# Joined key weights, wider complex products and an earlier token and modulation load in a one-core diffusion trunk

## The reference, cut to what matters

```python
def even_mixer(u_ctx, u_lat, w_in, w_out, ...):
    z = u @ w_in                                  # 27 tiles of 128 columns
    hyena: v, x1, x2 = conv3(z[:1536])            # two long convolutions by DFT:
        y = x1 * irfft(rfft(v) * rfft(filter_0))
        y = x2 * irfft(rfft(y) * rfft(filter_1))
    rwkv, 8 heads of 64, forward and backward over the tokens:
        S = S * w_t + (S @ -kk_t) outer (kk_t * a_t) + v_t outer k_t
        out_t = S @ r_t
    return concat(hyena, readout(rwkv)) @ w_out
```

## Time and profile before

| | |
|---|---|
| executions timed, median | 2153.88 us |
| the profiled execution | 2149.79 us, span 2148.0 us |
| mean granted TensorE clock | 0.973 |
| busy: TensorE, weight load, VectorE, ScalarE, GpSimd | 94%, 76%, 37%, 35%, 43% |
| first chunk products to first SwiGLU product | 34.6 to 72.5 us |
| even mixer's recurrence with its preparation | 684 to 867 us |

### The profile page before, as it was taken

How to read it: one execution, slowest core, us unless ns; L and a number is a source line. 1 busy time by engine, 2 the same in 40 slices (tenths; PEclk the granted TensorE clock), 3 DMA queues, 4 the chain that set the end, 5 groups by cost and what they waited for, 6 DMA issues and landing times.

```text
span 2148.0 us, 32168 instructions
## 1 busy us (share of the span) xinstructions
PE 2023.6 (94%) x13777; PEld 1621.7 (76%) x13777; DVE 799.1 (37%) x1158; ACT 752.2 (35%) x1060; POOL 919.4 (43%) x423
## 2 busy tenths in 40 slices
PE   5999999989999688889999998999999989989997
PEld 2677877768864577667788776777888869979996
DVE  3332032262237654363212224522133346546113
ACT  1512222254344332562222124522122275545343
POOL 0443443435413320443344444444444454448884
PEclk9999999999999799899999999999999999999998
DMA  9564336323320334326533543463232232225551
GB/s 323 181 210 153 119 106 223 121 79 137 108 49 12 73 71 104 132 94 206 195 108 108 196 157 108 133 223 124 79 118 78 69 124 79 80 79 157 196 182 55
DMA packets 232190, 276.53 MB, mean 129 GB/s; under 512 B 46725, under 2 KB 201491, under 8 KB 231732
## 3 DMA queue, kind: packets, MB, share of 16 engines
q1 hardware_dynamic: 228730, 268.65, 38.4%
q10 hardware_dynamic: 3322, 5.86, 0.8%
HBM read 265.05 MB, written 9.44 MB: 128 GB/s over the span
## 4 chain that ended last, share of the span: by engine, by line
PE 82%; DVE 6%; ACT 4%; issue 3%; DMA 2%; SPq 2%; POOL 1%; ACTq 0%; POOLq 0%; DVEq 0%
PE psum L1247 82%; DMA arena<-in_ada_w 1%; DMA arena<-in_x 1%; DVE rs L2087 1%; ACT arena L883 1%; SPq L672 0%; ACTq L795 0%; DVE h L2066 0%; ACT w_hi L854 0%; ACT L945 0%; DMA arena<-v_kept 0%; DVE arena L2175 0%; SPq L658 0%; ACT arena L1195 0%; DVE h L2134 0%
## 5 line engine op out<-in xcount | busy, mean ns | idle before, releaser
L2565 POOL TENSOR_TENSOR w_lo<-arena,w_hi 128x1024 fp32r<-128x1024 f32 x332 | 815.1, 2461 | 1011.5 <-ACT w_hi L854 1009.3
L1247 PE MATMUL psum<-u_hi,w_hi 128*128 128x512 f32 (+1 forms) x1888 | 699.3, 370 | 38.5 <-ACT u_hi L883 15.2
L1247 PE MATMUL psum<-u_hi,w_lo 128*128 128x512 f32 (+1 forms) x1888 | 689.5, 365 | 0.0
L1247 PE MATMUL psum<-u_lo,w_hi 128*128 128x512 f32 (+1 forms) x1888 | 675.2, 363 | 0.0
L854 ACT ACTIVATE w_hi<-arena 128x1024 fp32r<-128x1024 f32 x332 | 349.1, 1058 | 728.1 <-PE psum L1247 717.6
L1247 PEld LDWEIGHTS psum<-u_hi,w_hi 128*128 128x128 f32 x1888 | 363.1, 192 | 130.9 <-issue 28.6
L1247 PEld LDWEIGHTS psum<-u_hi,w_lo 128*128 128x128 f32 x1888 | 363.4, 192 | 54.7
L1247 PEld LDWEIGHTS psum<-u_lo,w_hi 128*128 128x128 f32 x1888 | 359.3, 191 | 53.4 <-issue 0.5
L2036 DVE TENSOR_TENSOR tmp<-psum,tmp 128x512 f32<-128x512 f32 (+1 forms) x88 | 55.0, 625 | 585.0 <-ACT tmp L908 585.0
L1247 PE MATMUL psum<-hid_hi,w_hi 128*128 128x512 f32 (+1 forms) x704 | 257.4, 366 | 1.7 <-POOL w_lo L2565 1.2
L1247 PE MATMUL psum<-hid_hi,w_lo 128*128 128x512 f32 (+1 forms) x704 | 255.3, 363 | 0.0
(11 more groups left out here) (259 smaller groups left out, 1478.8 us busy)
## 6 DMA issues: line engine op xcount, KB each, us to landing
arena<-in_ada_w SPq DMA_DIRECT2D x48, 1536.0 KB, 6.9
arena<-in_ffn_wg SPq DMA_DIRECT2D x44, 1024.0 KB, 5.5
arena<-in_ffn_wu SPq DMA_DIRECT2D x44, 1024.0 KB, 8.0
arena<-in_ffn_wd SPq DMA_DIRECT2D x20, 2048.0 KB, 8.8
arena<-in_ev_w_in SPq DMA_DIRECT2D x6, 2048.0 KB, 7.8
arena<-in_od_w_in SPq DMA_DIRECT2D x6, 2048.0 KB, 8.6
arena<-in_ffn_wd SPq DMA_DIRECT2D x4, 1024.0 KB, 5.0
arena<-inverse_kept SPq DMA_DIRECT2D x32, 128.0 KB, 3.0
```

Of the source, the lines that this page charges most:

```text
L1247: return pe.matmul(dst, w, x, start=first_, stop=last, skip_group_check=True)
L2565: pool.tensor_tensor(piece_shape(split_lo(pc), src), src, piece_shape(split_hi(pc).bitcast(F32), src), ALU.subtract).then_inc(S("lo_done"), 1)
```

## The change

It has five parts.

1. Loads: the token blocks are issued by SP, two at its very head and two behind the filter network's inputs; all eight modulation chunks are issued ahead of the first up weights. ScalarE issues the constants after its first sine, copies five token tiles, does the second sine, three more tiles and then the Silu of `c`; `ada_out(0)` goes ahead of `first_pieces`. TensorE makes `taps_of(1)` after two chunks in place of three.
2. Complex products: six operations of 128x1024 in place of twelve of 128x512.
3. Keys: both kinds lie side by side (`key_pairs`, two buffers each), so that one weight load has 128 columns. `both_kinds` has 8 matmuls in place of 16, `turn_keys` 16 in place of 32. The writers work on 64 partitions each (`key_slot`, `halves_of`): four operations for what two did. The values get a third buffer.
4. Decays are split in "keys" and "read" parts, those of pair 1 have homes of their own; the copy of the first rates goes (`rates` writes to `aa` itself).
5. Order: `strict(1)` comes ahead of `both_kinds(0, 0)`, which waits for it; `strict(2)` in step 0 and `strict(3)` at the end of step 2, in place of steps 1 and 3. `lanes(1)` is split over the doublings and step 0. The rates of pair 1 come before `lanes(0)`. SP's list of moves follows.

```diff
@@ the start: SP, ScalarE, TensorE
+            load_tokens(0)
+            load_tokens(1)
             load_filter("ld_mlp", zT, K["k_zT"])
...
             load_filter("ld_mlp", fw2, A["hy_f_w2"][0])
-            load_ada(0, 0)
+            load_tokens(2)
+            load_tokens(3)
...
-            for c in range(1, 6):
+            for c in range(AN):
                 load_ada(0, c)
             sp.wait_ge(S("ada_used"), 3)
             load_up("up_a", 0, 0, 0)
-            load_ada(0, 6)
-            load_ada(0, 7)
...
+            for k in range(KT):
+                if k == TOK_RING:
+                    act.wait_ge(S("sin_arg"), 2)
+                    act.activation(h2, pre, ACT.Sin).then_inc(S("sin_done"), 1)
+                act.wait_ge(S("tok_turned"), k + 1)
+                act.activation(hv[:, k], bank[1 + k % TOK_RING], ACT.Copy).then_inc(S("h_ready"), 1)
...
+            ada_out(0)
             first_pieces(0, 0, PIECES)
-            ada_out(0)
...
             ada(0, 1)
+            taps_of(1)
             ada(0, 2)
-            taps_of(1)
@@ VectorE, multiplied
+                    re, im = psum[:, 4 * s:4 * s + 2, :], psum[:, 4 * s + 2:4 * s + 4, :]
...
+                    ve.tensor_tensor(out_re, re, kre, ALU.mult).then_inc(S("ve_steps"), v.step())
+                    ve.tensor_tensor(ft, im, kim, ALU.mult).then_inc(S("ve_steps"), v.step())
+                    ve.tensor_tensor(out_im, re, kim, ALU.mult).then_inc(S("ve_steps"), v.step())
+                    ve.tensor_tensor(im, im, kre2, ALU.mult).then_inc(S("ve_steps"), v.step())
+                    ve.wait_ge(S("ve_steps"), v.n)
+                    ve.tensor_tensor(out_re, out_re, ft, ALU.subtract).then_inc(S("ve_steps"), v.step())
+                    ve.tensor_tensor(out_im, out_im, im, ALU.add).then_inc(S("ve_steps"), v.step())
@@ keys
-        bk0 = [by_tile(at) for at in (h[:, 0:1024], h[:, 1024:2048])]
-        bk1 = by_tile(h[:, 2048:3072])
+        key_pairs = [at.rearrange("p d c (i k t) -> p d c i k t", i=2, k=2)
+                     for at in (h[:, 0:2048].rearrange("p (d c x) -> p d c x", d=2, c=CT),
+                                big[:, 0:4096].rearrange("p (d c x) -> p d c x", d=2, c=CT)[:, :, :, 0:256])]
...
+        def key_slot(j, d, kind, e):
+
+            return key_pairs[j % 2][rows_of[e], d][:, :, :, kind ^ e]
...
                     for c in range(CT):
-                        for kind, key in enumerate((bk0[j % 2], bk1)):
-                            for e, rows in enumerate(rows_of):
-                                ins = mm(bank[factor_bank(n, d, e)][rows_of[e ^ kind], c * P:(c + 1) * P], key[rows, d, c, t],
-                                         two_kinds(rows, ar0[j % 3][:, d, c, t], ar1[j % 2][:, d, c, t]), True, True)
+                        for e, rows in enumerate(rows_of):
+                            ins = mm(bank[factor_bank(n, d, e)][:, c * P:(c + 1) * P], both_keys(d, c, n, rows),
+                                     two_kinds(rows, ar0[j % 3][:, d, c, t], ar1[j % 2][:, d, c, t]), True, True)
@@ both_kinds, waits of d == 0
-                        pe.wait_ge(S("a_done"), min(STEPS, n + 2 + n % 2) if n else 2)
-                        pe.wait_ge(S("slots_1"), 2 + 4 * j)
+                        pe.wait_ge(S("a_done"), 4 if n < 2 else 6 if n < 5 else 8)
+                        pe.wait_ge(S("slots_1"), 6 + 6 * j)
@@ GpSimd
+                pool.wait_ge(S("h_moves"), 144)
+                pool.wait_ge(S("bonus_k"), 4)
+                second_keys(0)
                 reads(0)
-                pool.wait_ge(S("h_moves"), 144)
                 pool.wait_ge(S("first_slots"), 7)
                 receives(1)
-                pool.wait_ge(S("rates"), 1)
-                pool.wait_ge(S("slots_0"), 4)
+                second_keys(1)
+                reads(1)
+                pool.wait_ge(S("first_slots"), 9)
+                pool.wait_ge(S("slots_0"), 6)
+                pool.wait_ge(S("zeroed"), 7)
                 pool.memset(arena[:, 2048:4096], 0.0).then_inc(S("zeroed"), 1)
@@ TensorE, VectorE: order of the steps
-                strict(1)
                 both_kinds(1, 0)
...
                     if ahead:
                         turn_keys(n + 2)
+                    if n == 0:
+                        strict(2)
...
-                lanes(0)
                 rates(0, 1, 2)
                 rates(1, 0, 1)
                 ve.wait_ge(S("ve_steps"), v.n)
                 ve.sem_inc(S("first_slots"), 1)
+                lanes(0)
@@ SP, values
-                if n >= 2:
-                    sp.wait_ge(S("o_mm"), n - 1)
+                if n >= 3:
+                    sp.wait_ge(S("o_mm"), n - 2)
+                elif n == 2:
+                    sp.wait_ge(S("slots_0"), 6)
```

More of the change, by code:

```diff
@@ L1037, in even_mixer @@
                 act.activation(chunk_decay, big[:, 0:4096].rearrange("p (x t) -> p x t", t=C)[:, :, C - 1], ACT.Exp, scale=-DECAY).then_inc(S("exped"), 1)
-                decays_of(0, 0)
-                decays_of(0, 1)
+                for part in ("keys", "read"):
+                    for d in range(2):
+                        decays_of(0, d, part)
+                for d in range(2):
+                    decays_of(1, d, "keys")
                 v_out(0)
@@ L1089, in even_mixer @@
                 keys_out(1)
-                act.wait_ge(S("zeroed"), 6)
+                act.wait_ge(S("zeroed"), 7)
                 z_out(0, 4)
+                for d in range(2):
+                    decays_of(2, d, "read")
                 z_out(0, 5)
                 act.wait_ge(S("hy_done"), 4)
-                act.wait_ge(S("first_slots"), 9)
-                act.activation(aa[0], a_first, ACT.Copy).then_inc(S("rates"), 1)
                 for n in range(STEPS):
@@ L1103, in even_mixer @@
                         z_out(n + 1, 4)
-                        if n in (0, 2):
-                            decays_of(n // 2 + 2, 0)
+                        if n in (1, 2):
+                            for d in range(2):
+                                decays_of(3, d, "keys" if n == 1 else "read")
                         z_out(n + 1, 5)
@@ L1575, in bonus_sum @@
                     mm(bank[SPARE[i]], blk[:, :], bonus[:, i * NT:(i + 1) * NT], True, True).then_inc(S("bonus_sum"), 1)
+                bonus_sum(0)
+                bonus_sum(1)
+                pe.wait_ge(S("hy_mul"), 4)
+                back_turned(1)
                 v_turn(2)
                 v_turn(3)
-                for i in range(4):
-                    bonus_sum(i)
+                bonus_sum(2)
+                bonus_sum(3)
+                strict(1)
                 def both_kinds(n, d):
@@ L2241, in even_mixer @@
                     ve.tensor_tensor(ar0[0][:, d], chunk(kk, ch), recv, ALU.mult).then_inc(S("first_slots"), 1)
-                    ve.tensor_tensor(bk0[0][:, d], chunk(rate[d], ch), key, ALU.mult).then_inc(S("first_slots"), 1)
+                    for e in range(2):
+                        ve.tensor_tensor(key_slot(0, d, 0, e), halves_of(chunk(rate[d], ch), e), halves_of(key, e), ALU.mult)\
+                            .then_inc(S("first_slots"), 1)
                 mask_of = maskc[:, M_STRICT:M_STRICT + 4].rearrange("p (d a) t -> p d a t", a=2)
@@ L2256, in even_mixer @@
                 take_strict(0)
-                ve.wait_ge(S("kd_f"), 9)
-                for d in range(2):
-                    ve.tensor_tensor(bk1[:, d], chunk(kd[d], chunk_of(d, 0)), decay_homes(0, d)[2], ALU.mult)\
-                        .then_inc(S("first_slots"), 1)
                 multiplied(1, 1)
```

244 lines of the change are left out of this document (133 added, 111 removed).

## The result

The changed kernel is slower: 2152.93 us (median of 20 runs, 2146.34 to 2159.92) against 2147.85 us for the kernel before (20 runs), a ratio of 1.0030 with an interval of [1.0021, 1.0039]. The forecast was 2128. The profiled execution of the changed kernel took 2155.02 us (span 2153.1), 2.1 above its median. That of the kernel before took 2149.79 us (span 2148.0), 1.9 above its median, so the two profiles can stand for the two kernels.

A forecast was written before the change was run, and what follows sets the result against it. TensorE, 94% busy, was taken as the bound, with room only at the start and around the recurrence. -8 - 11.5 - 6 = -25.5 gave 2128.4 as median (2124 profiled); eight in ten between 2112 and 2142.

The forecast's parts named there:

- Start, -8: First 66 us: earlier tokens and modulation chunks remove TensorE's waits; -8 us, bounds -4 and -10.
- gives back 1.5: Start: weights landing last at 55 to 56 delay `filter_out(1)` to 75.6, past TensorE's second pair at 74; 1.5 us lost.
- Wide products, -1.4 each: Complex products before the recurrence: six operations at pitch 1.14 make 7.1 us; -1.4 us each, bounds -1.0 and -2.
- GpSimd's queue up to `strict(1)`: Ahead of the recurrence: GpSimd's 20 operations take 27.2 us from 687, so `strict(1)` starts at about 714.3.
- `both_kinds(0, 0)` at 717 less the start's gain, 709: Ahead of the recurrence: VectorE's earlier finish becomes a GpSimd wait; gain 0 up to this call.
- Into the first step, -11.5: From `both_kinds(0, 0)` to the first new state, at 739.1 against 750.62: -11.5 us, bounds 0 and -15.
- Steps, -6: Steps 0 to 6 of the recurrence, six spans between states that took 97.1 us: -6, bounds +2 and -10.
- Joined weights, 0: Recurrence: halving the count of key products with 128-column weights brings nothing to the time.
- The four switches of shape a step: Recurrence: changing TensorE's tiling mode drains the engine, at 0.18 us, costing 2.9 us and not more.
- Rival 2: GpSimd decides again: half-width operations cost 1.5 us or more, recurrence gain shrinks to -6; 2140 us, chance 0.13.
- Rival 4: Slower by the clock: TensorE stays at 1.2 GHz through the steps; 2168 us, chance 0.07 with any other loss.
- cases 3 and 4: Case 3: recurrence yields nothing, 2146 us, chance 0.07; case 4: slower by the clock, 2168 us, 0.07 with other losses.

The follow-up runs named there:

- a_turn: The changed kernel with the turned keys alone split again into 64-column weight loads: 2153.86 us, ratio 1.0027 to the kernel before.
- a_turn_hold3: The changed kernel with turned keys split again and GpSimd's work for pair 3 held until VectorE's lanes of pair 2 are through: 2146.94 us, ratio 1.0008.
- a_hold3: The changed kernel with GpSimd's twelve operations for chunk pair 3 held until VectorE's lanes of pair 2 are through: 2141.55 us, ratio 0.9977 to the kernel before.
- a_split: The changed kernel with all joined products (turned keys and both-kinds) split again into 64x64 tiles: 2154.25 us, ratio 1.0021 to the kernel before.
- the three pairs: Changed kernel, turned keys split, all joins split, each without and with pair 3's GpSimd work held: ratios 1.0030 to 0.9977, 1.0027 to 1.0008, 1.0021 to 0.9991.

## Why the prediction was wrong, step by step

The forecast counted from 2153.88 us, the median of three executions; over 20 the kernel before takes 2147.85. That offset of 6 us is not the error: the change was to bring -25.5 us and brought +5.1.

- **Start, -8: sized too high, measured -4.5.** TensorE's steps came as told: tokens at 17.23 (18.4 told), taps 23.60 (25.5), response 36.44 (38.4), `first_pair` 64.61 (63.0 told). The last chunk was waited for all the same (2.73 us). What was undersized is the "gives back 1.5": ScalarE waited 3.95 us for the first weights until 58.68 (55 to 56 told), so `filter_out(1)` ended at 79.1 and not at 75.6, and the second pair began 79.24 against 83.56: -4.3.
- **Wide products, -1.4 each: right where nothing ran beside them.** Pitch 1.13, a whole 7.0 us. In the last two wholes (7.8 and 7.2 us) the subtraction, which has both inputs in SBUF, took 1.97 and 1.46 us beside GpSimd in place of 1.23.
- **GpSimd's queue up to `strict(1)`: right.** 27.2 us told, 27.3 taken (684.59 to 711.9); `strict(1)` at 712.05 (714.3 told); half the partitions take the same time, 1.26 to 1.31 us where VectorE does not hold them up.
- **`both_kinds(0, 0)` at 717 less the start's gain, 709: the step that failed.** It came at 725.29. The working took `first_slots` 7 at 699.5 and gave VectorE its old durations beside a GpSimd that it had just made continuous. Rates took 5.87 us in place of 1.29 and `lanes(0)` 15.7 in place of 6.6: 13.7 us (by chance the number of the whole loss). In the profiled executions of a_turn and a_turn_hold3 the same call came at 720, so it is 11 to 16 us late by this forecast; 2.8 us of the difference is TensorE's lower clock ahead of the rates, which the working had not either. I counted GpSimd as a queue, with bounds on *its* durations; these held. It was the neighbour that grew. And between `strict(1)` and `both_kinds(0, 0)` stands `take_strict(1)` in VectorE's queue, behind those lanes: I asked who is ready, not who has to copy.
- **Into the first step, -11.5: measured -5.** From `both_kinds(0, 0)` to the first state 28.3 us (33.3 before, 22.1 told). The wait of `turn_keys(2)` for GpSimd's keys did go (one of 1.85 us stands before `strict(2)`), and ScalarE's fell from 3.3 to 0.8. Against that, the first calls ran at the lower clock (3.78 us for 32 records), and the turned keys took 2.58, 2.00 and 2.00.
- **Steps, -6: measured +7.1.** Again company: the one span with pair 3's products beside the lanes grew by 9.6 us, and with them held (a_hold3) it took 13.9 in place of 24.4. The next grew by 4.0 at the lower clock, and the other four shrank by 6.4 together. The hint stood in the trace of before, where GpSimd's last read ran from 779.11 to 780.38:

```profile
779.21 1.19 DVE L2349 TENSOR_TENSOR h<-h 128x8 f32<-128x8 f32 x1
780.43 0.17 DVE L2351 TENSOR_TENSOR h<-h 128x8 f32<-128x8 f32 x1
```

- **Joined weights, 0: right in the total, wrong in a size.** `both_kinds` keeps 1.11 to 1.16 us with x16 records. `turn_keys` does not: 2.00 us in place of 1.11. Its 32 loads of 128 columns are busy for 1.86 us of that, and the 16 of `both_kinds` for 0.97, about 60 ns each in both; that the loads set the pace is read from this and not tested by itself. It is 6.8 us of TensorE over eight calls, and taking it away gained nothing (a_turn). The four switches of shape a step, put at 2.9 us, do not show either: a_split, which takes them out of `both_kinds` too, stands at 1.0021, a_turn at 1.0027.
- **The sum.** In the two profiled executions `both_kinds(0, 0)` came 8.0 us later, the stretch to the first state gave back 5.0, the six spans lost 7.1, and the last step gave back 3.1 (the sums of the group norm begin at 875.70 where they began at 868.63). The rest of the kernel gave 2.0, and the spans differ by 5.1.
- **Rivals.** None was this one. Rival 2 named the two engines, with the price on the wrong one. Rival 4's clock (0.87 over 747 to 867, 0.64 over 780 to 810) answers the waits and adds to them; it did not begin them.

Two slips of the working change nothing: the profiled 2149.79 is not the fastest shown (2149.6 is), and half of cases 3 and 4 is 0.07, not 0.05.

What stays open: how much of the recurrence part's 13.7 us belongs to step 1 (4 to 11 by the three pairs), since each cure moves where TensorE waits and with it where the clock falls; and what the stretch before the recurrence would give if its lanes did not collide and nothing else moved, for which no kernel was found.

## What to carry to other kernels

When work moves to another engine or another place, look at what runs *beside* its new place, not only at its queue: a chain of short dependent VectorE products with both inputs in SBUF can pay a whole GpSimd product for each link (beside products that follow each other without a gap; where they wait for each other, about every other link got through). Bound the neighbour's durations as well as those of the moved work. Where two engines collide, an added wait on the one with slack can be the gain (here 4 to 11 us).

## What the runs showed of the hardware that was not expected

- Beside back-to-back GpSimd products of 1.23 to 1.31 us, all but one of VectorE's eight products of 8 elements in `lanes(0)` and step 1 took 1.17 to 1.21 us in place of 0.17, while reductions (0.28, 0.69) and operations with a PSUM input (1.21 for 128x1024, 1.29 for two of 128x512) kept their time.
- One VectorE operation of 0.69 us with two SBUF inputs took 4.20 us, past three GpSimd products, and GpSimd products beside VectorE's wider ones took up to 2.04.
- Beside GpSimd memsets, products kept their 0.17 us; copies of 128x8 took up to 0.90 (one run).
- Products of 64*128 tiles with 64 moving columns took 62 ns each (2.00 / 32), with their loads busy for 1.86 of the 2.00 us; with 128 moving columns and half the loads the call takes 1.11 to 1.16 us.
- After a wait of 3.69 us (a_turn_hold3) TensorE's granted clock was 0.50, and its next 270 small products took 13.25 us where 272 took 7.62 after a wait of 2.03.
